# Modulation sections in halves at the start of a two-layer diffusion backbone on one Trainium2 core

## The reference, cut to what matters

```python
m_l = silu(c) @ w_mod[i] + b_mod[i]          # the same for c_ctx: m_c
sh1, sc1, g1, sh2, sc2, g2 = split(m_l, 6)   # each 1024 wide
a_l = rmsnorm(x, norm_mix_g[i]) * (1.0 + sc1) + sh1
q, k, v, g = split(a_l @ gla_w_in)
gate = (a_l @ gla_gate_w1) @ gla_gate_w2 + gla_gate_b
```

## Time and profile before

| | us |
|---|---|
| median of 3 runs | 1690.49 (1689.52 to 1690.5) |
| the profiled execution, its own time | 1686.04 |
| its span, first to last instruction | 1684.1 |
| TensorE busy | 1614.6 |
| VectorE, ScalarE, GpSimd busy | 595.8, 522.3, 599.4 |

### The profile page before, as it was taken

The page is one execution under the profiler, slowest core; times in us unless marked ns, Lnnn a source line. Parts: engine busy times, 40 slices in busy tenths (PEclk is TensorE's granted clock), DMA queues, the critical chain, the costliest instruction groups (busy, mean ns, idle before and its releaser), DMA issues. The chain is left out here.

```text
span 1684.1 us, 22699 instructions
## 1 busy us (share of the span) xinstructions
PE 1614.6 (96%) x10014; PEld 1350.8 (80%) x10014; DVE 595.8 (35%) x711; ACT 522.3 (31%) x578; POOL 599.4 (36%) x433
## 2 busy tenths in 40 slices
PE   6999999998899999999999999899978999999997
PEld 3788797977788888888888887788866788888886
DVE  4453333453431121111211214869987321121122
ACT  4444243322231211111101122478873421122222
POOL 2122212212242242332322424245474444555442
PEclk9999999999999999999999999999999999999999
DMA  9324233322233333333332422121213233223322
GB/s 332 89 89 123 78 100 115 87 76 70 81 101 100 104 99 98 96 105 100 101 100 67 128 82 76 51 68 58 76 50 100 76 100 101 87 90 99 99 82 81
DMA packets 199317, 160.64 MB, mean 95 GB/s; under 512 B 7234, under 2 KB 193972, under 8 KB 199220
## 3 DMA queue, kind: packets, MB, share of 16 engines
q1 hardware_dynamic: 198832, 159.08, 30.6%
q10 hardware_dynamic: 388, 0.12, 0.0%
HBM read 157.08 MB, written 2.10 MB: 95 GB/s over the span
## 5 line engine op out<-in xcount | busy, mean ns | idle before, releaser
L510 POOL TENSOR_TENSOR w_lo<-raw,w_hi 128x512 fp32r<-128x512 f32 (+1 forms) x396 | 564.0, 1455 | 1056.0 <-ACT w_hi L1055 1056.0
L569 PE MATMUL duo<-a_hi,w_hi 128*128 128x512 f32 (+1 forms) x1584 | 466.3, 356 | 22.4 <-DVE a_lo L1525 15.5
L572 PE MATMUL duo<-a_lo,w_hi 128*128 128x512 f32 (+1 forms) x1584 | 460.9, 353 | 0.0
L575 PE MATMUL duo<-a_hi,w_lo 128*128 128x512 f32 (+1 forms) x1584 | 460.1, 352 | 0.0
L1055 ACT ACTIVATE w_hi<-raw 128x2048 fp32r<-128x2048 f32 (+1 forms) x99 | 188.6, 1905 | 540.8 <-PE duo L575 535.7
L569 PEld LDWEIGHTS duo<-a_hi,w_hi 128*128 128x128 f32 x1584 | 258.1, 190 | 75.7 <-issue 31.3
L572 PEld LDWEIGHTS duo<-a_lo,w_hi 128*128 128x128 f32 x1584 | 258.0, 190 | 42.6
L575 PEld LDWEIGHTS duo<-a_hi,w_lo 128*128 128x128 f32 x1584 | 257.6, 190 | 42.8
L1759 DVE TENSOR_TENSOR hid<-duo,gate 128x1024 f32<-128x1024 f32 (+1 forms) x33 | 33.5, 1043 | 522.5 <-PE duo L575 522.5
L575 PE MATMUL duo<-h_hi,w_lo 128*128 128x512 f32 (+1 forms) x528 | 160.7, 356 | 0.0
L569 PE MATMUL duo<-h_hi,w_hi 128*128 128x512 f32 (+1 forms) x528 | 159.9, 355 | 0.0
(11 more groups left out here) (275 smaller groups left out, 1585.9 us busy)
## 6 DMA issues: line engine op xcount, KB each, us to landing
raw<-in_ffn_w_dram SPq DMA_DIRECT2D x120, 512.0 KB, 4.8
mod_ring<-in_w_mod_dram SPq DMA_DIRECT2D x80, 512.0 KB, 5.3
raw<-in_gla_w_in_dram SPq DMA_DIRECT2D x24, 512.0 KB, 4.7
raw<-in_lru_w_in_dram SPq DMA_DIRECT2D x16, 512.0 KB, 4.2
raw<-in_ffn_w_dram SPq DMA_DIRECT2D x16, 384.0 KB, 3.8
mod_first<-in_w_mod_dram SPq DMA_DIRECT2D x4, 1024.0 KB, 14.6
mod_second<-in_w_mod_dram SPq DMA_DIRECT2D x4, 1024.0 KB, 14.3
raw<-in_gla_w_out_dram SPq DMA_DIRECT2D x8, 512.0 KB, 5.0
```

Of the source, the lines that this page charges most:

```text
L510: pool.tensor_tensor(w_lo[b][:, k:k + 2, 0:cols], raw[b][:, k:k + 2, 0:cols], w_hi[b][:, k:k + 2, 0:cols].bitcast(F32), ALU.subtract).then ...
L569: pe.matmul(tile_out(ps, t, part, n), wh, act_hi[:, k, s:s + n], start=opens, stop=False, skip_group_check=True)
L572: pe.matmul(tile_out(ps, t, part, n), wh, act_lo[:, k, s:s + n], start=False, stop=False, skip_group_check=True)
L575: mm = pe.matmul(tile_out(ps, t, part, n), wl, act_hi[:, k, s:s + n], start=False, stop=last, skip_group_check=True)
```

## The change

Sections 1 and 0 are loaded and used in four pieces of 2 MB, each half a section: piece 0 is scale columns 0 to 511, piece 1 shift columns 0 to 511, pieces 2 and 3 their second halves. All are in rows of 2 KB. SyncE's order is pieces 0 and 1, gate1, q/k, pieces 2 and 3, then as before; the first two ring loads no longer wait for `mod_used`. Even pieces use `mod_psum`, odd ones `vec_psum`.

TensorE does the products of pieces 0 and 1, their turns, the norm sums, the products of piece 2, and then k-row 0; behind it the turn of piece 2 and the products of piece 3, and behind k-row 1 the turn of piece 3. The waits for gate1 and q/k are by pair of k-rows, and the low-rank products of the context start at k = 3, four at once.

ScalarE loads the silu table first; the Ln/Exp table follows the first two copies. The high halves of gate1 and q/k stand ahead of Ln and Exp, the copy of piece 2 ahead of a_hi's row 1, that of piece 3 ahead of row 3, and v's high half right behind row 7. gate1 has buffers of its own (`gate1_hi`, `gate1_lo`). VectorE makes section and gain in halves, the second ones ahead of rows 3 and 4 of its loop, and clears gate2 before the sums of squares.

```diff
@@ -188,8 +188,10 @@
-        mod_first = place("mod_first", [P, 8, D], F32, H_AT)
-        mod_second = [place("mod_second0", [P, 8, 512], F32, A_AT), place("mod_second1", [P, 8, 512], F32, H_AT + 32 * KB)]
+        mod_start = [place(f"mod_start{i}", [P, 8, 512], F32, offset)
+                     for i, offset in enumerate((A_AT, A_AT + 16 * KB, H_AT, H_AT + 24 * KB))]
+        gate1_hi = place("gate1_hi", [P, 8, P], F32R, H_AT + 40 * KB)
+        gate1_lo = place("gate1_lo", [P, 8, P], F32R, H_AT + 16 * KB)
...
@@ -363,7 +364,8 @@
                 for p in pieces:
-                    sp.wait_ge(mod_used, 8 * (s - SEC_HEAD) + p + 1)
+                    if (s, p) not in ((SEC_HEAD, 0), (SEC_HEAD, 1)):
+                        sp.wait_ge(mod_used, 8 * (s - SEC_HEAD) + p + 1)
@@ -374,17 +376,16 @@
             w_first = w_mod[0].rearrange("(k p) n -> p k n", p=P)
...
+            def start_piece(i):
+                c0 = SEC_FIRST[i % 2] * D + i // 2 * 512
                 for k in range(0, KT, 4):
...
+                    sp.dma_start(mod_start[i][:, k:k + 4], w_first[:, k:k + 4, c0:c0 + 512]
+                                 ).then_inc(start_loaded[i][k // 4], 16)
+            start_piece(0)
+            start_piece(1)
@@ -407,7 +408,8 @@
             qk_load(0)
-            second_half(1)
+            start_piece(2)
+            start_piece(3)
@@ -503,14 +505,17 @@
...
+            def low(ch):
                 b = ch % 2
                 pool.wait_ge(hi_ready, ch + 1)
                 for k in range(0, 8, 2):
...
-            low(0, P)
...
+            pool.wait_ge(hi_ready, 1)
+            for k in range(0, 8, 2):
+                pool.tensor_tensor(gate1_lo[:, k:k + 2], raw[0][:, k:k + 2, 0:P], gate1_hi[:, k:k + 2].bitcast(F32),
+                                   ALU.subtract).then_inc(lo_ready, 1)
@@ -693,22 +698,27 @@
...
+            def start_products(i):
+                if i >= 2:
+                    pe.wait_ge(half_ready, i - 1)
+                for k in range(KT):
+                    if k % 4 == 0:
+                        pe.wait_ge(start_loaded[i][k // 4], 16)
+                    g = 32 * (k % 4)
+                    mm = pe.matmul((mod_psum, vec_psum)[i % 2][g:g + 32, :], cs[:, k], mod_start[i][:, k], start=k < 4,
+                                   stop=k >= 4, tile_position=(0, g), skip_group_check=True)
+                mm.then_inc(start_used if i < 2 else mod_used, 1)
+            def start_turn(i):
+                pe.wait_ge(mod_rowed, i + 1)
+                if i == 0:
+                    pe.wait_ge(pick_made, 1)
+                for p in range(4):
+                    at_ = 512 * (i % 2) + p * P
+                    mm = pe.matmul((mod_psum, vec_psum)[i % 2][:, 2 * p:2 * p + 2], first_rows[:, at_:at_ + P], pick[:],
                                    start=True, stop=True, skip_group_check=True)
                 mm.then_inc(mod_turned, 1)
...
@@ -719,27 +729,16 @@
             pe.wait_ge(cs_ready, 1)
...
-            first_turn(0, 0)
-            first_turn(0, 1)
+            start_products(0)
+            start_products(1)
+            start_turn(0)
+            start_turn(1)
             norm_sums(0, BOTH)
-            pe.wait_ge(mod_ready, 1)
-            second_products(0)
-            first_turn(1, 0)
-            second_products(1)
-            first_turn(1, 1)
-
-            chunk_wait("gate1")
-            chunk_wait(("qk", 0))
+            start_products(2)
+            pe.wait_ge(hi_ready, CH[("qk", 0)] + 1)
             duo_wait(("qk", 0))
-            hi, lo = w_hi[CH["gate1"] % 2], w_lo[CH["gate1"] % 2]
+            hi, lo = gate1_hi, gate1_lo
@@ -751,13 +750,22 @@
                 a_wait(("prep", 0, 0))(k)
+                pair_wait("gate1", k)
                 low_rank(k, 0)
-                for j in ((), (), (0, 1, 2), (3,), (4,), (5,), (6,), (7,))[k]:
+                pair_wait(("qk", 0), k)
+                if k == 3:
+                    pe.wait_ge(mod_ready, 2)
+                for j in ((), (), (), (0, 1, 2, 3), (4,), (5,), (6,), (7,))[k]:
                     mm = low_rank(j, 1)
                 if k == KT - 1:
                     done(mm)
                 for t in range(2):
                     mm = tile_row(("qk", 0), ("qk", 0), BOTH, a_hi, a_lo, 8, k, t, begin=t == 0)
+                if k == 0:
+                    start_turn(2)
+                    start_products(3)
+                elif k == 1:
+                    start_turn(3)
@@ -1052,7 +1060,8 @@
                     wait_done(act, q_before)
-                act.activation(w_hi[b][:, 0:rows, 0:cols], raw[b][:, 0:rows, 0:cols], ACT.Copy).then_inc(hi_ready, 1)
+                act.activation(gate1_hi[:] if name == "gate1" else w_hi[b][:, 0:rows, 0:cols], raw[b][:, 0:rows, 0:cols],
+                               ACT.Copy).then_inc(hi_ready, 1)
@@ -1105,13 +1114,12 @@
                 if n == 0:
-                    first_copy(1, 0)
-                    high("gate1", None, P)
-                    high(("qk", 0))
-                    act.wait_ge(half_ready, 1)
+                    act.wait_ge(half_ready, 2)
                 for m in range(KT):
                     if n == 0 and m == 1:
-                        first_copy(1, 1)
+                        start_copy(2)
+                    if n == 0 and m == 3:
+                        start_copy(3)
@@ -1147,13 +1155,15 @@
             rows(r1[V_LAM:V_LAM + 16], lru_lambda.rearrange("j d (m p) -> (j d m) p", p=P))
...
+            act.preload_act_table_set("silu_and_others")
+            def start_copy(i):
+                if i < 2:
+                    act.wait_ge(start_used, i + 1)
                 else:
...
+                    act.wait_ge(mod_used, i - 1)
+                    act.wait_ge(mod_turned, i - 1)
+                act.activation(first_rows[:, i % 2 * 512:(i % 2 + 1) * 512], (mod_psum, vec_psum)[i % 2][:], ACT.Copy
@@ -1166,15 +1176,18 @@
                            ACT.Silu).then_inc(cs_ready, 1)
-            act.preload_act_table_set("natural_log_exp_and_others")
             for n in range(4):
                 if n == 2:
                     x_copy(3)
                 wait_moved(act, ("turn", n))
                 square(0, n, BOTH)
-            first_copy(0, 0)
-            first_copy(0, 1)
+            start_copy(0)
+            start_copy(1)
+            act.preload_act_table_set("natural_log_exp_and_others")
+            high("gate1", None, P)
+            high(("qk", 0))
             prep(0, 0, BOTH)
+            high(("v", 0))
@@ -1183,7 +1196,6 @@
             moved(act.activation(t_low[:, LAT:TOK], vec_psum[0:64, 0:CTX], ACT.Copy), "tlow")
-            high(("v", 0), "tlow")
...
@@ -1466,30 +1472,40 @@
+            def start_section(i):
+                dve.wait_ge(mod_turned, i + 1)
+                row, c0 = SEC_FIRST[i % 2], 4 * (i // 2)
+                bias = V_BMOD + 8 * row + c0
+                dve.tensor_tensor(mod[:, row, c0:c0 + 4],
+                                  (mod_psum, vec_psum)[i % 2][:, 0:8].rearrange("p (m v) -> p m v", v=2),
+                                  vec[:, 0, bias:bias + 4].unsqueeze(2).broadcast_to([P, 4, 2]),
+                                  ALU.add).then_inc(half_ready if i < 2 else mod_ready, 1)
+            def start_gain(h):
+                dve.wait_ge(mod_ready if h else half_ready, 1)
+                steps.link(dve.scalar_tensor_tensor(out=gain[:, 0, 4 * h:4 * h + 4], in0=mod[:, SEC_FIRST[0], 4 * h:4 * h + 4],
+                                                    scalar=1.0,
+                                                    in1=vec[:, 0, V_NMIX + 4 * h:V_NMIX + 4 * h + 4].unsqueeze(2).broadcast_to(
+                                                        [P, 4, 2]), op0=ALU.add, op1=ALU.mult))
             def prep(layer, which, parts):
                 n = 2 * layer + which
                 width = parts[-1][1] + parts[-1][2]
                 g = vec[:, 0, (V_NMIX if which == 0 else V_NFFN) + 8 * layer:][:, 0:8]
                 sec = 6 * layer + 3 * which
-                dve.wait_ge(mod_ready, [1, 6, 8, 11][n])
...
+                if n == 0:
+                    start_section(0)
+                    start_gain(0)
+                    start_section(1)
+                    dve.wait_ge(half_ready, 2)
+                else:
+                    dve.wait_ge(mod_ready, [1, 6, 8, 11][n])
+                    steps.link(dve.scalar_tensor_tensor(out=gain[:, n], in0=mod[:, sec + 1], scalar=1.0,
+                                                        in1=g.unsqueeze(2).broadcast_to([P, 8, 2]), op0=ALU.add,
+                                                        op1=ALU.mult))
                 wait_done(dve, ("stat", n))
                 dve.wait_ge(rooted, ROOTED[n] + len(parts))
...
@@ -1503,8 +1519,11 @@
                 for m in range(KT):
-                    if n == 0 and m == 2:
-                        second_section(1)
+                    if n == 0 and m == 3:
```

(45 more changed lines are left out.)

22 lines of the change are left out of this document (removed).

## The result

The changed kernel takes 1680.3 us (median of 5, 1679.79 to 1681.09) against 1690.49 (1688.1 to 1693.23), a ratio of 0.9944 with a 95% interval of 0.9933 to 0.9956. On a second chip it took 1681.06 (1680.42 to 1682.23) against 1689.45 of the kernel before, 0.9953 (0.9941 to 0.9966).

The account below looks back on a forecast made before the run. TensorE, busy for 96% of the span, was taken as the bound. The start's 2.7 us plus the v projection's 2.0 gave 4.7 us, taken off the 1690.49 us median: 1685.8 us, range 1682.1 to 1689.9.

Parts of the forecast that it names:

- The data: Start loads: with 2 MB less ahead, q/k lands at 29.9 for 34.7; the fourth piece lands at 40.6.
- D: Start loads: gate1's issue has its own price, q/k lands near 33, 3.1 us are gone; 1688.9 us, chance 0.17.
- E: ScalarE's queue at the start: late q/k delays row 0 one for one; 1693.6 us if at 36.0, chance 0.09.
- Row 0: First dense k-row on TensorE: starts at 37.6 instead of 44.41, 6.8 us earlier, with ScalarE as the path.
- they end near 31: Start: pieces 1 and 2, their copies, turns and norm sums end near 31, under q/k's transfer, and cost nothing.
- Into the dense stretch: TensorE between rows 0 and 2: two turns and a piece's products come in, 4.1 us, with no wait added.
- The clock at row 0: TensorE at row 0: 1.2 GHz expected again for 3.9 us of dense work, costing 1.95 us.
- Case A: The forecast as worked out, with 1.2 GHz at row 0 costing 1.95 us; 1685.8 us, chance 0.42.
- case B: TensorE's clock is up at row 0 or comes back at once, so 1.95 us goes; 1683.8 us, chance 0.12.
- C: 1.2 GHz holds a further stretch over the turn, products and row 1, costing 1.7 us; 1687.5 us, chance 0.20.
- v: v projection: its 2.91 us wait goes, 0.9 is lost at ScalarE's table load, 2.0 gained; bounds 1.0 to 2.9.
- The sum: Whole kernel: 2.7 us from the start plus 2.0 from v, 4.7 us, taken equally off profiled execution and median.

Follow-up runs that it names:

- a_copy: The changed kernel, without further edits, run again on a second chip; 1681.06 us, ratio 0.9953 to the kernel before.
- a_sums1st: The changed kernel with the norm sums ahead of the turns of pieces 0 and 1; 1682.74 us, ratio 0.9961 to the kernel before.
- a_fillstart: The changed kernel with one 512-column product in each of two DMA waits of pieces 0 and 1; 1681.32 us, ratio 0.9963 to the kernel before.
- a_order: The changed kernel with the turns of pieces 2 and 3 and products of piece 3 back ahead of row 0; 1685.11 us, ratio 0.9978.
- a_vlate: The changed kernel with v's high half late again, behind the copies of the low-rank product; 1687.57 us, ratio 0.9985 to the kernel before.
- b_gatebuf: The kernel before with gate1's own buffers and v's high half behind row 7; 1684.47 us, ratio 0.9967 to the kernel before.
- b_copy: The kernel before, unchanged, run and traced again; 1689.84 us, ratio 0.9997.

## Why the prediction was right in sign and wrong in size

- **The data.** Right. q/k landed at 29.2 (forecast 29.9): its second load was issued at 22.9 and landed 6.3 later; in a_copy it landed at 28.2. The fourth piece landed at 40.1 (40.6), issued at 26.6 with 13.5 to landing. gate1's second issue still took 7.3 us, but it was over at 19.6. So rivals D and E, q/k late, did not come.
- **Row 0.** 38.57 for 37.6. A path that the forecast had wrong, worth 1.0 us: "they end near 31". The sums ended at 33.3, TensorE was at 1.2 GHz from 20.7 to 34.3, and Ln waited 1.45 us for them. With the sums ahead of the turns (a_sums1st) Ln does not wait and row 0 starts at 37.60, the forecast's time. That the waits for DMA between the halves of pieces 0 and 1 bring the low clock is not shown. a_fillstart fills two of the three, and Ln does not wait; but nor does it in a_order, where TensorE's program is the same up to there, nothing is filled and the clock fell some 4 us later.
- **Into the dense stretch.** Right: a turn 1.0 to 1.3, products 1.92, a turn 0.95, 4.2 us for 4.1 by their durations (3.9 in the first trace and 3.6 in a_copy's from their starts to those of what follows), and no wait of TensorE in between. a_order shows that the order is worth what it costs.
- **The clock at row 0.** Case A in one trace, case B in the other. In the first, 1.2 GHz lasted through row 0 and into the turn, to about 44.5, and cost 2.7 us (2.4 in row 0, 0.3 in the turn) where the forecast has 1.95; that is between A and C. Stage 1 gained 1.2 and 3.9; forecast 2.7. The medians put the start between 1.9 us (a_vlate against before) and 3.4 (a_copy against b_gatebuf), 2.4 to 2.5 by the ratios, so this term was near. The Trainium skill (TensorE: Matmul & The Clock Gate, section HAM oscillation) tells of matmul groups that each start at the half rate behind a wait for a DMA. The wait ahead of row 0 was one for VectorE's a_lo, of 2.78 and 2.71 us: behind the first row 0 started slow, behind the second it did not.
- **v.** The term that was mis-sized: 2.0 us in the sum. The move itself is 1.74 us (28.05 to 26.31), but b_copy, with the mean clock of most executions of before, spends 30.75 us there, so the term is 4.4 by the traces, and 5.0 in the median of b_gatebuf. That 1.74 lies near 2.0 is luck. The forecast lets all 2.91 us go and loses 0.9 at ScalarE's table load. In fact v still waits 1.17 us for `zg`, starts 1.74 earlier, and loses nothing at the table load, which ends at 91.77, 0.3 before v_tok can start. The prediction saw the 2.91 us wait, priced the wait, and did not ask what TensorE's clock does behind it, though it weighed that very question for row 0.
- **The sum.** The sentence that hid the error is "a difference of the start is the same in both". It was not: the low clock in v stood in the median and not in the trace. The 4.4 us between the profiled execution and the median were the one sign, in the rows shown, that the trace was not a typical execution. With 1.2 to 3.9 from stage 1 and 4.4 from stage 2 the gain is 5.6 to 8.3; measured are 10.2 on the first chip and 8.4 (7.9 by the ratio) on the second. The last 2 us on the first chip stand beside a rest of 1582.4 us in its trace, 2 to 4 less than in any other trace; why is open, and a second trace of the same kernel had 1585.5.

## What to carry to other kernels

Where the profiled execution is faster than the median of the runs by more than the runs differ, ask what it lacks before summing from it; the mean granted clock of many executions shows whether it may be the clock, and a second trace shows where. Price an idle gap of TensorE as the gap itself and, if the clock may fall behind it, as what the work behind it loses: here 1.7 us, and 2.7 of the 5.9 us of v that ran at 1.2 GHz. A filler test (work in the gap that computes nothing) separates the two, if its runs are compared by their clock as well as by their time.

## What was not expected of the hardware

- A wait of 2.9 us, with thin matmuls of 32 rows or 32 columns ahead of it, came with 6.8 us at 1.2 GHz in one trace of a kernel and with none in another, with the gate matmuls and the end of the wait within 0.03 us of each other. One trace cannot show whether a gap costs the clock; the mean clock over many runs can.
- With twelve matmuls in the gap the clock stayed up in all three traces. Where they added no wait of their own the stage was as short (28.1 us) as in the one trace in which the clock stayed up with the gap empty.
- TensorE stood at 1.2 GHz while it was busy without a break: 3.40 of 3.40 us in each window from 24.1 to 34.3, with turns of two columns, norm sums and 32-column products.
- Row 0 started at 38.57 and 38.53 in two executions and took 5.3 and 2.9 us.
